# A two-block sequence model on one core: twelve column units of the second projection by Strassen's seven products, and a recurrence moved beside the row blocks

## The chip, the cores and the metric

The kernel runs on one core of a Trainium2 chip, as one launch. The metric is the device time of that launch in microseconds (us), lower is better. Engine names are those of the profile: PE is TensorE, with PEld for its weight loads, DVE is VectorE, ACT is ScalarE, POOL is GpSimd and SP is SyncE, which here only issues DMAs.

## What is computed

Two blocks run one after the other on 2048 tokens of width 1024, in float32. The first is a pooling mixer with a residual and two norms. The second, where the change lies, projects its normed and modulated input `h` to 4624 columns and feeds two mixers:

```python
proj = h @ w_in + b_in                       # (2048 x 1024) @ (1024 x 4624)
(na_q, na_k, na_v, na_z, ml_q, ml_k, ml_v, ml_o, ml_z,
 i_f, f_f, i_b, f_b) = split(proj)           # nine blocks of 512 columns and 16 gate columns
na_out = neighbourhood_attention(na_q, na_k, na_v, rpb) * silu(na_z)
mq, mk = silu(short_conv(ml_q, ml_k))        # five taps along the tokens
h_fwd = mlstm_chunkwise(mq, mk, ml_v, i_f, f_f)
h_bwd = flip(mlstm_chunkwise(flip(...)))
y = concat(na_out, norm((h_fwd + h_bwd) * sigmoid(ml_o)) * ml_norm_w * silu(ml_z)) @ w_out
```

`mlstm_chunkwise` carries a state from chunk to chunk: `C_new = decay * C + v_c^T k_c`. That is the recurrence of the title.

## The kernel before

There is no scheduler. Each engine has a program written out by hand, one Python method for each engine of each stage (`sp`, `act`, `dve`, `pool`, `pe`), and the engines meet by counting semaphores: `w.wait_ge(*self.full.ge(n + 1))` holds the engine that runs it, and all that stands behind it on that engine. An engine's instructions run in the order in which they are written.

**Products.** Every float32 operand is held as a high and a low part, and each product of 128 x 128 x 512 takes three matmuls (`mm3`, L143, matmuls L145 to L147): high by high, high by low, low by high.

**The second projection** (`Proj`, L1209). `self.work` is the list of its items, one PSUM bank each. The nine blocks go by names: nq, nk, nv, nz for the attention, mq, mk, mv, mo, mz for the other mixer. A block of 512 columns is four units of 128 columns. An item is either one unit by 512 tokens, or, for the row blocks mv, nv and mo, all four units by 128 tokens (16 items for a block). Both take 8 x 3 = 24 matmuls of 512 columns. The order is nq, nk, mv, mk, mq, the 16 gate columns, nv, nz, mz, mo. Items before `nv0` use eight PSUM banks in turn, later ones five; the other three belong to the recurrence. Units of weights sit in six slots in SBUF. `load` (L1371, on SP) brings a unit's raw weights into one of two buffers `iraw`, `split_high` (L1403, ACT) and `split_low` (L1440, DVE) make its two parts, and a unit's loads stand in `after[n]`, behind the item `n` that frees its slot.

**Reading out.** DVE adds the bias to a row item (L1653, `row_step`). For mq and mk ACT adds the bias and DVE runs the five taps (L1618). Items of nv are stored by SP itself: it waits for the item's `row_step` and then issues four DMAs into `VM`, or six into `VM` and `VE` at every second item (L1496, L1498). All other stores are POOL's.

**The recurrence** (`States`, L2249) has 31 steps, one after each item from `s0` on. In step s, SP loads a chunk of keys into the one buffer `skC` (L2312, once the last chunk was transposed) and of values into `sv` (L2322), and stores the state of step s - 2 (L2327). POOL weighs the values (L2378), PE multiplies (L2397) and, in the first 16 steps, transposes the keys (L2409), and DVE updates the state (L2358). Before it come the `Gates` steps (L2111), which begin at `g0`. PE's part after item n is, cut:

```python
s = n - self.s0 - 1                       # product of the step before
... w.wait_ge(*self.weighed.ge(i + 1)) ... matmuls L2397
s += 1                                    # transposes of this step
if 0 <= s < NT:
    w.wait_ge(*self.k_in.ge(s + 1))       # keys of step s = n - s0 have landed
    ... four transposes L2409
```

and SP's part after item n issues the load of step s = n - s0, behind whatever SP does for item n of the projection. In the kernel before, `g0 = nv0 + 3` and `s0 = nv0 + 21`: the 31 steps stand beside items 5 to 15 of nz, all of mz and the first items of mo.

The attention (`Attention`, L1770) starts inside the last item of mo with the work of its first two pairs (`first_pe`, `first_act`, `first_dve`, `first_pool`); its inputs are loaded beside mo (`early_sp`, L1864), and POOL prepares its masks there (`block`, L2010).

Of the kernel before, what the change touches and what calls it, by code (L numbers as in the profile page):

```python
# [10 lines left out]
P = 128  # L11
# [1193 lines left out]
BLOCKS = [("nq", 0), ("nk", 1), ("mv", 6), ("mk", 5), ("mq", 4), ("nv", 2), ("nz", 3), ("mz", 8), ("mo", 7)]  # L1205
# [3 lines left out]
class Proj:  # L1209


    NU = 6
# [3 lines left out]
    def __init__(self, k, banks, out, gw):  # L1216
        self.k, self.out, self.gw = k, out, gw
        NU = self.NU
# [9 lines left out]
        self.cu = [k.at(f"cu{i}", 168 + 2.03125 * i, [P, 4 + W + 2]) for i in range(2)]  # L1228
        self.ca = [k.at(f"ca{i}", 172.0625 + 2.03125 * i, [P, W + 2]) for i in range(2)]
        self.br, self.wgr = k.at("br", 178.125, [P, 2, W]), k.at("wgr", 182.125, [P, KT, 16])  # L1230

        self.wg = k.at("wg", 176.125, [P, KT, 48], F32R)
# [8 lines left out]
        self.conv_u, self.conv_out, self.row_step, self.sign = k.sem("conv_u"), k.sem("conv_out"), k.sem("row_step"), k.sem("sign")  # L1241
# [3 lines left out]
        self.cols = [b * W + j * P for _, b in BLOCKS for j in range(4)]  # L1245
        work = []
        for bi, (name, b) in enumerate(BLOCKS):
            u0 = 4 * bi
            if name == "nv":
                work += [("gates", 0, tb) for tb in range(TB)]  # L1250
            if name in ROW_BLOCKS:
                work += [(name, u0, m) for m in range(NT)]
            elif bi == 0:
                work += [(BLOCKS[u // 4][0], u, tb) for tb in range(TB) for u in range(NU)]
            else:
                units = range(u0 + 2, u0 + 4) if bi == 1 else range(u0, u0 + 4)
                work += [(name, u, tb) for u in units for tb in range(TB)]
        self.work = work

        jobs = [("h", 0, 0), ("h", 0, 1), ("h", 0, 2), ("h", 0, 3), ("w", 0), ("w", 1)]  # L1260
        self.early = {12: (0, 2), 13: (2, 4), 14: (4, 5), 15: (5, 6)}
        self.ahead, self.after, nu = {}, {}, NU
        for n, (name, u, tb) in enumerate(work):
            first = len(jobs)
            if n == 0:
                jobs += [("w", 2), ("w", 3)]
            elif n < 3:
                jobs.append(("w", n + 3))
            if 2 <= n < 6:
                jobs.append(("h", 1, n - 2))  # L1270
            if n == 3 * NU:
                jobs.append(("gates",))
            if NU <= n < 3 * NU and u < 4:
                jobs.append(("h", tb + 1, u))
            self.ahead[n] = (first, len(jobs))
            first = len(jobs)
            last_of_unit = name not in ROW_BLOCKS and name != "gates" and tb == 3
            last_of_rows = name in ROW_BLOCKS and tb == NT - 1
            more = u + 1 + NU if last_of_unit else u + 4 + NU if last_of_rows else 0
            while nu < min(more, 36):  # L1280
                jobs.append(("w", nu))
                nu += 1
# [5 lines left out]
        self.freed = {}  # L1288
        for n, (name, u, tb) in enumerate(work):
            if name == "gates":  # L1290
                continue
            for x in range(4 if name in ROW_BLOCKS else 1):
                self.freed[u + x] = n + 1


        self.stage, nst, self.convs = {}, 0, {}
        for n, (name, u, tb) in enumerate(work):
            if name in ("mq", "mk"):
                self.convs[n] = len(self.convs)
            else:  # L1300
                self.stage[n] = nst
                nst += 2 if name in ("nq", "nk") else 1
        self.users = {}
        for n, i in self.stage.items():
            self.users[i] = n
            if work[n][0] in ("nq", "nk"):
                self.users[i + 1] = n

        self.evac_at, self.row_at, self.sign_at, c = {}, {}, {}, 0
        for n, (name, u, tb) in enumerate(work):  # L1310
            c += {"nq": 4, "nk": 1, "nz": 1, "mz": 1, "gates": 1, "mo": 1}.get(name, 0)
# [152 lines left out]
    def sp(self, e, att, states):  # L1464
        k, io, out, work = self.k, self.k.io, self.out, self.work
        w = Waits(e)
        for n, (name, u, m) in enumerate(work):
# [31 lines left out]
            for x in range(*self.after[n]):  # L1499
                self.load(e, w, x)  # L1500
# [1611 lines left out]
```

## Time and profile before

| | |
|---|---|
| runs | 1884.83, 1886.8 and 1890.14 us, median 1886.8 |
| span of the profiled execution | 1883.3 us (the page gives no other time of it; the median of the runs is 3.5 us longer) |
| busy: PE, PEld, DVE, ACT, POOL | 99%, 82%, 52%, 33%, 29% of the span |
| granted PE clock | 0.999 of full speed over the span |
| first projection item to last | from 598 to 1442 us of the span |
| waits of PE for another engine | 12, the longest 1.8 us |

A busy share is the part of the span in which an engine had an instruction running. In a view of waits, "A <- B" says that engine A sat idle until B's instruction released it. In the chain of work each piece is what the next one waited for. A DMA's "to landing" is from its issue to its data being there.

### The profile page before, as it was taken

How to read it: one execution, taken by the hardware profiler on the slowest of the kernel's cores; microseconds unless marked ns; L12 is line 12 of the kernel's file. 1: busy time of each engine (PE TensorE's matmuls, PEld its weight loads, DVE VectorE, ACT ScalarE, POOL GpSimd, SP SyncE). 2: the span in 40 equal slices, each digit the busy share in tenths (PEclk: the TensorE clock that was granted, in tenths of full speed). 3: DMA queues.
4: the chain of work that ended last, by engine and by line, in shares of the span. 5: the costliest groups of instructions: out<-in, count | busy, mean ns of one | idle time of the engine just before them, and what ended most of it. 6: DMA issues, size and time to landing. Idle time of an engine off the chain costs nothing.

```text
span 1883.3 us, 26698 instructions
## 1 busy us (share of the span) xinstructions
PE 1865.6 (99%) x10035; PEld 1540.4 (82%) x10035; DVE 982.4 (52%) x2117; ACT 618.3 (33%) x1317; POOL 552.5 (29%) x925
## 2 busy tenths in 40 slices
PE   9999999999999999999999999999999999999998
PEld 8888878888888888888888787888887777788886
DVE  6556565775666433114777322223213777776665
ACT  7321111233444432101222202221114667655552
POOL 2112222233642222110110000222314777544442
PEclk9999999999999999999999999999999999999999
DMA  6223142366897745312221123665563776867663
GB/s 197 95 79 119 62 128 81 104 184 235 306 266 252 235 168 162 101 50 84 74 78 68 53 62 116 211 211 171 168 220 105 243 232 224 271 219 241 230 229 112
DMA packets 236365, 303.55 MB, mean 161 GB/s; under 512 B 41414, under 2 KB 161126, under 8 KB 236204
## 3 DMA queue, kind: packets, MB, share of 16 engines
q1 hardware_dynamic: 205724, 215.84, 37.4%
q0 software_dynamic: 23600, 77.61, 11.4%
q10 hardware_dynamic: 6912, 8.39, 1.2%
q8 instruction: 80, 1.31, 0.3%
q14 instruction: 49, 0.40, 0.1%
HBM read 194.71 MB, written 107.54 MB: 160 GB/s over the span
## 4 chain that ended last, share of the span: by engine, by line
PE 94%; DVE 2%; DMA 2%; issue 1%; ACT 1%; POOL 0%; SPq 0%; POOLq 0%; DVEq 0%; ACTq 0%
PE banks L145 25%; PE banks L147 25%; PE banks L146 25%; PE banks L2106 3%; PE banks L2069 3%; PE banks L2088 3%; PE banks L2704 2%; PE banks L2706 1%; PE banks L2397 1%; DMA iraw<-in_w_in 1%; PE banks L2089 1%; PE banks L2674 1%; PE banks L234 1%; PE banks L1109 1%; PE banks L1741 0%
## 5 line engine op out<-in xcount | busy, mean ns | idle before, releaser
L145 PE MATMUL banks<-hT,wu 128*128 128x512 f32 (+1 forms) x528 | 204.6, 387 | 1.1 <-DVE wu L512 0.6
L147 PE MATMUL banks<-hT,wu 128*128 128x512 f32 (+1 forms) x528 | 202.3, 383 | 0.0
L146 PE MATMUL banks<-hT,wu 128*128 128x512 f32 (+1 forms) x528 | 202.2, 383 | 0.0
L145 PE MATMUL banks<-iT,wub 128*128 128x512 f32 x384 | 151.2, 394 | 0.0
L145 PE MATMUL banks<-iT,wua 128*128 128x512 f32 x384 | 150.8, 393 | 0.0
L145 PE MATMUL banks<-wub,iT 128*128 128x512 f32 x384 | 150.6, 392 | 0.0
L147 PE MATMUL banks<-iT,wub 128*128 128x512 f32 x384 | 149.7, 390 | 0.0
L147 PE MATMUL banks<-iT,wua 128*128 128x512 f32 x384 | 149.5, 389 | 0.0
L146 PE MATMUL banks<-wub,iT 128*128 128x512 f32 x384 | 149.5, 389 | 0.0
L147 PE MATMUL banks<-wub,iT 128*128 128x512 f32 x384 | 149.5, 389 | 0.0
L146 PE MATMUL banks<-iT,wua 128*128 128x512 f32 x384 | 149.5, 389 | 0.0
L146 PE MATMUL banks<-iT,wub 128*128 128x512 f32 x384 | 149.4, 389 | 0.0
L1653 DVE TENSOR_TENSOR st<-banks,br 128x512 f32<-128x512 f32 x48 | 33.1, 692 | 201.0 <-PE banks L147 193.5
L145 PEld LDWEIGHTS banks<-hT,wu 128*128 128x128 f32 x528 | 99.3, 188 | 25.3 <-ACT ub L470 4.3
L147 PEld LDWEIGHTS banks<-hT,wu 128*128 128x128 f32 x528 | 99.2, 188 | 19.6
L146 PEld LDWEIGHTS banks<-hT,wu 128*128 128x128 f32 x528 | 99.3, 188 | 18.5
L1932 ACT ACTIVATE p<-s,ast 128x480 f32<-128x480 f32 (+1 forms) x128 | 83.7, 655 | 53.0 <-DVE ast L1970 53.0
L145 PE MATMUL banks<-ws,ys 128*128 128x512 f32 x256 | 100.5, 393 | 0.0
L147 PE MATMUL banks<-ws,ys 128*128 128x512 f32 x256 | 99.8, 390 | 0.0
L146 PE MATMUL banks<-ws,ys 128*128 128x512 f32 x256 | 99.7, 389 | 0.0
L1618 DVE SCALAR_TENSOR_TENSOR ca<-cu,cw,ca 128x512 f32<-128x512 f32 (+2 forms) x128 | 96.3, 752 | 4.5
L2039 POOL TENSOR_SCALAR p<-p,ast 128x384 f32<-128x384 f32 (+1 forms) x128 | 71.9, 562 | 46.2 <-DVE ast L1976 44.8
(293 smaller groups left out, 4116.3 us busy)
## 6 DMA issues: line engine op xcount, KB each, us to landing
iraw<-in_w_in SPq DMA_DIRECT2D x36, 512.0 KB, 4.4
wa<-in_w_ada SPq DMA_DIRECT2D x48, 256.0 KB
yT<-sg POOLq DMA_DIRECT2D x32, 256.0 KB, 3.1
oraw<-yT SPq DMA_DIRECT2D x32, 256.0 KB, 4.8
xr<-in_x SPq DMA_DIRECT2D x16, 512.0 KB, 4.4
h<-h POOLq DMA_DIRECT2D x16, 512.0 KB, 4.3
hT<-tr POOLq DMA_DIRECT2D x16, 512.0 KB, 5.1
tws<-wg SPq DMA_DIRECT2D x16, 512.0 KB, 5.1
```

What stands on the lines that cost most here:

```text
L145: e.matmul(ps, lh, rh, start=first, stop=False)
L146: e.matmul(ps, lh, rl, start=False, stop=False)
L147: return e.matmul(ps, ll, rh, start=False, stop=last)
L234: t = e.transpose(self.tp[m][g][:, j * P:(j + 1) * P], self.x[m][:, (4 * g + j) * P:(4 * g + j + 1) * P], self.ident[:])
L1618: e.scalar_tensor_tensor(out=a[:, left:right], in0=cur[:, left + x:right + x], scalar=cw[:, x, ch:ch + 1], in1=a[:, left:right], op0=ALU.m ...
L1653: e.tensor_tensor(self.st[i % 2][:], pb, self.br[:, x % 2, :], ALU.add).then_inc(*self.row_step.inc())
L1932: e.activation(self.pr[n % 8][:, 0:N], self.sr[n % 4][:, 0:N], ACT.Exp, bias=self.st[:, n, 0:1], scale=-1.0, accum_out=self.st[:, n, 1:2]) ...
L2039: e.tensor_scalar(rows[:, :, 0:P], rows[:, :, 0:P], self.st[:, n, 2:3], 1.0, ALU.mult, ALU.mult).then_inc(*self.scaled.inc())
L2069: t = e.matmul(self.pS[(2 * p + hh) % 4][:, 0:N], b[r, q, (2 * i + a) * P:(2 * i + a + 1) * P], keys, start=x == 0, stop=x == 2)
L2088: e.transpose(self.pT[x][:, j * P:(j + 1) * P], probs[:, 160 * j:160 * j + P], self.ident[:])
L2106: t = e.matmul(self.pO[d, 0:P], v, self.ptr[(2 * q + hh) % 4][r, j * P:(j + 1) * P], start=(j == 0), stop=(j == nb))
L2704: t = e.matmul(o, self.eb[c % 2][d][:, h, :], self.v1[c % 2][:, h, :], start=True, stop=not self.inter(c, d))
```

## The change

It does three things.

1. **Order of the projection.** A table `PLAN` gives the units' order: nz first (with the gate columns after each group of four items), then mk, mq, mv, mq, nv, mq, mo. nq, nk and mz, twelve units together, leave the list, which is now 100 items long. The weight slots follow a table `SLOT`.
2. **The recurrence** begins one item after mv begins (`g0`), its steps 18 items later (`s0`): item 63 and on, so beside the last item of mq2 (items 60 to 63), nv (64 to 79), mq3 (80 to 83) and mo (84 to 99, up to item 93).
3. **Fast**, a new class. nq, nk and mz are taken as 2 x 2 blocks (two halves of the inner dimension, two units, two token blocks of 512) and multiplied by Strassen's seven products, each 12 matmuls of 512 columns; there are 84 products in 6 rounds of 14. Three of the sums of weights and three of the sums of tokens are made in DRAM: SP copies one operand to `wsum` or `hsum`, and POOL issues a DMA that adds the other (15 of each). The other sums, and the high and low parts, are made on DVE and ACT. Attention's early work moves to the last products.

```diff
+PLAN = [("nz", 0), ("nz", 1), ("nz", 2), ("nz", 3), ("mk", 0), ("mk", 1), ("mk", 2), ("mq", 0), ("mq", 1), ("mk", 3),
...
+        work = [x for tb in range(TB) for x in [(PLAN[u][0], u, tb) for u in range(4)] + [("gates", 0, tb)]]
+        for u in range(4, len(PLAN)):
+            name, j = PLAN[u]
             if name in ROW_BLOCKS:
+                work += [(name, u, m) for m in range(NT) if j == 0]
             else:
+                work += [(name, u, tb) for tb in range(TB)]
...
-        self.nv0 = nv0 = next(n for n, x in enumerate(work) if x[0] == "nv")
-        self.place = [n % 8 if n < nv0 else (nv0 + (n - nv0) % 5) % 8 for n in range(len(work))]
+        self.g0 = g0 = next(n for n, x in enumerate(work) if x[0] == "mv")
+        self.place = [n % 8 if n < g0 else (g0 + (n - g0) % 5) % 8 for n in range(len(work))]
...
     def sp(self, e, fast, states):
...
             if name == "nv":
                 i = self.stage[n]
...
                 w.wait_ge(*self.row_step.ge(self.row_at[n]))
                 for y in range(2):
...
                         e.dma_start(k.VM[:, 40 * r4:40 * r4 + nc, m // 2, a, :].rearrange("hp c d -> c hp d"), src).then_inc(*self.v_st[i % 2].inc())
...
             for x in range(*self.after[n]):
                 self.load(e, w, x)
+            fast.copy(e, w, n - 22)
             states.sp(e, w, n)
             if name == "mo":
-                att.early_sp(e, w, m)
+                fast.early_sp(e, w, m)
...
             out.tail_pool(e, w, n)
+            fast.add(e, w, n - 36)
             states.pool(e, w, n)
...
+class Fast:
+    N, ND, OUTS, SLOTS = 84, 6, 48, 10
+    SEQ = [(i, q) for i, q in ((5, 0), (5, 1), (2, 0), (2, 1), (1, 0), (3, 0), (1, 1), (3, 1), (4, 0), (4, 1), (6, 0), (6, 1), (7, 0), (7, 1))]
+    DOUBLES = [(("nq", 0), ("nk", 0)), (("nq", 2), ("nk", 2)), (("mz", 0), ("mz", 2))]
+    ORDER = [(0, 0), (0, 1), (0, 2), (1, 2), (1, 0), (1, 1)]
...
+    def copy(self, e, w, n):
+        if 0 <= n < 9:
+            b, x = divmod(n, 3)
+            e.dma_start(self.ws[b, x], self.columns(b, (0, 0, 1)[x], 0)).then_inc(*self.copy_in.inc())
+        elif 9 <= n < 15:
+            half, x = divmod(n - 9, 3)
+            e.dma_start(self.hs[half, x], self.tokens(half, self.LEFT[self.LONG[x]][0])).then_inc(*self.copy_in.inc())
+
+    def add(self, e, w, n):
+        if 0 <= n < 9:
+            b, x = divmod(n, 3)
+            w.wait_ge(*self.copy_in.ge(15))
+            e.dma_start(self.ws[b, x], self.columns(b, (1, 0, 1)[x], 1), accum_op=ALU.add).then_inc(*self.added.inc())
...
+    def early_act(self, e, w, m):
+        if m in self.early_x:
+            self.tokens_high(e, w, *self.early_x[m])
+        if m == NT - 1:
+            for j in range(4):
+                self.weights_high(e, w, j)
...
+    def act(self, e, att):
+        for j in range(self.N):
...
+            elif j in self.at:
+                self.high(e, w, self.at[j])
+            if j + 4 < self.N:
+                self.weights_high(e, w, j + 4)
...
+    def pe(self, e, att):
+        for j in range(self.N):
...
+            for c in range(KT // 2):
+                e.matmul(ps, t[:, 0, c], x[:, 0, c], start=new and c == 0, stop=False, skip_group_check=not new)
+                e.matmul(ps, t[:, 0, c], x[:, 1, c], start=False, stop=False, skip_group_check=not new)
+                m = e.matmul(ps, t[:, 1, c], x[:, 0, c], start=False, stop=c == KT // 2 - 1, skip_group_check=not new)
+            m.then_inc(*self.full.inc())
...
     def early_sp(self, e, w, m):
-        if m == 11:
-            w.wait_ge(*full)
+        if m == 80:
+            w.wait_ge(*fast.full.ge(m))
             for j in self.jobs:
                 if j[0] == "t":
                     self.load(e, w, 0, j)
...
-        self.g0 = proj.nv0 + 3
-        self.s0 = proj.nv0 + 21
+        self.g0 = proj.g0 + 1
+        self.s0 = self.g0 + 18
```

How the order of instructions moves shows at three places. First, the program of SP beside the recurrence. `skC` and `sv` are its loads of keys and values, `CD` the store of the state. Before, with nz and mz as the items:

```order
L2312 DMA skC_158<-mk 128x4x128 [waits s_turned_236]
L2322 DMA sv_160<-mv 128x4x128 [waits s_weighed_238]
L2327 DMA CD<-state_162 128x516 [waits updated_240]
L1389 DMA iraw_178_134<-in_w_in 128x8x128 [waits i_lo_208]
L2312 DMA skC_158<-mk 128x4x128 [waits s_turned_236]
```

and now, beside two items of nv (L1490 and L1492 are the stores that were L1496 and L1498, L2742, L2752 and L2757 the recurrence):

```order
L1490 DMA VM<-st_189_145 40x4x128 [waits row_step_217]
L1490 DMA VM<-st_189_145 40x4x128
L1490 DMA VM<-st_189_145 8x4x128
L1492 DMA VE<-st_189_145 32x512
L1490 DMA VM<-st_189_145 8x4x128
L1492 DMA VE<-st_189_145 32x512
L2742 DMA skC_158<-mk 128x4x128 [waits s_turned_235]
L2752 DMA sv_160<-mv 128x4x128 [waits s_weighed_237]
L2757 DMA CD<-state_162 128x516 [waits updated_239]
L1490 DMA VM<-st_188_144 40x4x128 [waits row_step_217]
L1490 DMA VM<-st_188_144 40x4x128 x3
L2742 DMA skC_158<-mk 128x4x128 [waits s_turned_235]
```

The load of keys stood behind waits of the recurrence and of weight buffers; it now stands behind the wait for the current item's row add and that item's stores. Second, PE at the end of an item of nv in the change:

```order
L147 MATMUL banks<-wub_133,iT_172_128 128x512
L2825 MATMUL banks<-swv_161,skT_159 128x129 [waits updated_239,kt_out_236,s_weighed_237]
L2825 MATMUL banks<-swv_161,skT_159 128x129
L2825 MATMUL banks<-swv_161,skT_159 128x129 [waits updated_239]
L2825 MATMUL banks<-swv_161,skT_159 128x129
L2837 MATMUL banks<-ident_58,skC_158 128x128 [waits sk_in_229]
L2837 MATMUL banks<-ident_58,skC_158 128x128 x3
L145 MATMUL banks<-wub_133,iT_172_128 128x512 [waits biased_212]
```

The order on PE is that of before, with a row item in the place of a column item: the product of one step, then the transposes of the next, then the next item. Third, SP behind the last item of nv in the change (L1382 loads a unit of weights; before, four such loads stood there too, and no `sv` behind them):

```order
L1492 DMA VE<-st_189_145 32x512
L1382 DMA iraw_178_134<-in_w_in 128x8x128 [waits i_lo_208]
L1382 DMA iraw_179_135<-in_w_in 128x8x128 [waits i_lo_208]
L1382 DMA iraw_178_134<-in_w_in 128x8x128 [waits i_lo_208]
L1382 DMA iraw_179_135<-in_w_in 128x8x128 [waits i_lo_208]
L2752 DMA sv_160<-mv 128x4x128 [waits s_weighed_237]
```

The values for the recurrence's next product are loaded behind four loads of weights, two of which wait for buffers.

## Rows read from the trace of the kernel before

**Rows 1.** The page's head, the busy line of PE and the granted clock
```profile
span 1883.3 us, 26698 instructions
PE 1865.6 (99%) x10035; PEld 1540.4 (82%) x10035; DVE 982.4 (52%) x2117; ACT 618.3 (33%) x1317; POOL 552.5 (29%) x925
PEclk9999999999999999999999999999999999999999
```

**Rows 2.** Windows: PE, PEld, DVE, ACT, POOL busy, clock, DMA share, GB/s
```profile
600.00:615.00 15.00, 13.98 (x70) 11.50 (x69) 10.26 (x13) 8.65 (x16) 2.74 (x5) 1.00 1.06 353
900.00:1000.00 100.00, 100.00 (x443) 82.81 (x442) 72.34 (x123) 26.77 (x42) 10.50 (x19) 1.00 0.21 72
1140.00:1165.00 25.00, 23.24 (x104) 18.93 (x103) 6.48 (x9) 7.48 (x8) 1.33 (x3) 1.00 0.50 141
```

**Rows 3.** Timeline of DVE in nv: start, duration, and idle before with its releaser
```profile
1064.36 0.69 DVE L1653 TENSOR_TENSOR st<-banks,br 128x512 f32<-128x512 f32 x1 [4.75 <-PE banks L147]
1069.79 0.69 DVE L1653 TENSOR_TENSOR st<-banks,br 128x512 f32<-128x512 f32 x1 [4.75 <-PE banks L147]
```

**Rows 4.** Chain of work, window 1140 to 1170: start, duration, piece
```profile
1142.22 0.25 PE banks L147
1142.49 0.70 DVE st L1653
1143.21 0.27 SPq L1496
...
1145.06 0.32 SPq L1498
1145.42 0.42 SPq L1389
1145.88 5.25 DMA iraw<-in_w_in
1151.16 1.07 ACT wub L1438
1152.26 1.24 DVE wub L1443
1153.51 4.35 DMA iraw<-in_w_in
1157.88 1.07 ACT wub L1438
1158.98 1.23 DVE wub L1443
```

**Rows 5.** Timeline of SP in nv, an item with four DMAs
```profile
1070.51 1.54 SPq L1496 DMA_DIRECT2D VM<-st  x4
1072.21 1.15 SPq L2134 DMA_DIRECT2D I<-gt  x2
```

**Rows 6.** Line L2312, the load of keys: issue in ns min/median/max, and to landing
```profile
L2312 SPq DMA_DIRECT2D skC<-mk x16: 359/360/372, 1169.8 to 1273.6; - x16
...
DMA to landing us min/median/max: 2.5/3.2/3.8
```

**Rows 7.** Chain of work, whole span: two products of the recurrence
```profile
1183.70 0.89 PE banks L2397 x8
1190.52 0.89 PE banks L2397 x8
```

**Rows 8.** Timeline of POOL: a wait for values, and their weighing
```profile
1199.74 1.05 POOL L2378 TENSOR_TENSOR swv<-sv,wT 128x516 f32<-128x516 f32 x1 [0.79 <-DMA sv<-mv]
```

**Rows 9.** Line L2322, the load of values: issue in ns, and to landing
```profile
L2322 SPq DMA_DIRECT2D sv<-mv x30: 529/530/1432, 1170.2 to 1370.9; - x30
...
DMA to landing us min/median/max: 3.0/3.4/4.8
```

**Rows 10.** PE's waits, 1100 to 1180, and the page's group of conv taps
```profile
PE banks L2240 <- DVE dg L2213: 1.8, 1, 1.8
...
L1618 DVE SCALAR_TENSOR_TENSOR ca<-cu,cw,ca 128x512 f32<-128x512 f32 (+2 forms) x128 | 96.3, 752 | 4.5
```

**Rows 11.** DMA issues: count, KB each, median us to landing
```profile
rpbp<-in_rpb POOLq DMA_DIRECT2D x1, 465.0 KB, 4.5
...
mv<-st POOLq DMA_DIRECT2D x16, 256.0 KB, 2.3
```

**Rows 12.** Timelines of ACT, POOL, SP and PE where the attention takes over
```profile
1436.27 0.63 ACT L1578 ACTIVATE st<-st 128x512 f32<-128x512 f32 x1 [4.81 <-DVE st L1653]
1436.91 1.28 ACT L1932 ACT_TABLE_LOAD   x1
...
1437.73 1.92 POOL L2017 COPY mid<-tab 128x960 f32<-128x960 f32 x2
1439.71 3.12 POOL L2024 MEMSET mid<- 32x640 f32 x7
...
1419.21 4.47 SPq L1852 DMA_DIRECT2D tab<-Z  x8
...
1443.05 1.59 PE L2069 MATMUL banks<-hd 64*128 64x480 f32 x12 [0.78 <-DVE st L1653]
```

More of the change, by code:

```diff
@@ L1287, in __init__ @@
         self.rawn = {n: i for i, n in enumerate(n for n, j in enumerate(jobs) if j[0] != "gates" and n not in self.passing)}
[L1288 to L1296, printed above, removed]
+        self.stage, self.convs = {}, {}
         for n, (name, u, tb) in enumerate(work):
@@ L1300, in __init__ @@
             else:
[L1301 to L1309, printed above, removed]
+                self.stage[n] = len(self.stage)
+        self.users = {i: n for n, i in self.stage.items()}
+        self.evac_at, self.row_at, c = {}, {}, 0
         for n, (name, u, tb) in enumerate(work):
-            c += {"nq": 4, "nk": 1, "nz": 1, "mz": 1, "gates": 1, "mo": 1}.get(name, 0)
+            c += name in ("nz", "gates", "mo")
             self.evac_at[n] = c
@@ L1429, in split_high @@
             u = j[1]
-            if u >= self.NU:
-                w.wait_ge(*self.full.ge(self.freed[u - self.NU]))
+            if self.prior[u] is not None:
+                w.wait_ge(*self.full.ge(self.freed[self.prior[u]]))
             elif u >= 2:
@@ L1472, in sp @@
                     self.pass_load(e, w, 1, x)
-            if n == 5:
+                w.wait_ge(*out.modulated.ge(NT))
+                e.dma_start(self.wgr[:], self.win[:, :, 36 * P:36 * P + 16]).then_inc(*self.wg_in.inc())
+            if n == 4:
                 for x in range(4):
@@ L1542, in act @@
                 else:
-                    w.wait_ge(*out.modulated.ge(NT))
+                    w.wait_ge(*self.full.ge(self.freed[1]))
                 e.activation(cu[:, 4:4 + W], pb, ACT.Identity, bias=bc[:, bcol:bcol + 1]).then_inc(*self.biased.inc())
@@ L1891, in sp @@
         proj, states = self.proj, self.states
-        w.wait_ge(*proj.full.ge(len(proj.work)))
+        w.wait_ge(*self.fast.full.ge(self.fast.N))
         for i in range(2):
             w.wait_ge(*proj.ca_st[i].ge(16))
-        for name in ("mv", "mz", "mo"):
+        for name in ("mv", "mo"):
             proj.stored_all(w, name)
-        w.wait_ge(*proj.row_step.ge(48))
+        self.fast.stored(w, self.fast.OUTS)
+        self.fast.read(w)
         states.stored_all(w)
@@ L2295, in sp @@
         if n == self.g0 - 1:
-            for i in range(2):
-                w.wait_ge(*proj.ca_st[i].ge(16))
             proj.stored_all(w, "gates")
@@ L2362, in pool @@
         if n == self.g0 - 1:
-            for i in range(2):
-                w.wait_ge(*self.proj.ca_st[i].ge(16))
             self.g.consts(e, w)
@@ L2383, in pe @@
             for b in self.proj.reserved:
-                self.proj.read_out(w, max(x for x in range(self.proj.nv0) if self.proj.place[x] == b))
+                self.proj.read_out(w, max(x for x in range(self.proj.g0) if self.proj.place[x] == b))
         self.g.pe(e, w, n - self.g0)
@@ L2995, in whole @@
         mixer = Mixer(k, hT, banks, norm)
+        over = [x for x in k.used[first:] if x not in (mixer.full, mixer.y_step)]
         out = FirstOut(k, banks, mixer, ident, mhalf)
         gw = GatedWeights(k, out)
-        ended = k.used[first:]
+        ended = [x for x in k.used[first:] if x not in over]
         proj = Proj(k, banks, out, gw)
         states = States(k, proj, ident)
-        att = Attention(k, proj, states, ident)
         with k.nc.Block() as block:
```

602 lines of the change are left out of this document (472 added, 130 removed).

## The prediction

> **What bounds the kernel now.** The page's first lines come first: PE is busy for 1865.6 of 1883.3 us and its clock is full in every slice, while the next engine, DVE, reaches 52% [rows 1]. So time goes only where PE does less, or where it is made to wait. The windows say where it waits in the projection: never in the conv items, where DVE is busy for 72 of 100 us; 1.0 us at the start and 1.8 us behind nv [rows 2]. The reader is to see that PE is the whole bound and that any wait of PE adds its full length. Next comes PE's pace: the row adds of two successive items of nv start 5.43 us apart [rows 3], 24 matmuls, so 0.226 us a matmul.
>
> The last view decides this case. The chain of work behind the last item of nv runs: last matmul ends (1142.47), DVE adds the bias, SP issues six stores, and only then the next load, at 1145.42 [rows 4]. SP's program is in order: what stands behind a row item's stores starts 2.95 us after the item's last matmul. Today nothing that PE needs soon stands there for nv.
>
> **The change part by part.** Twelve units took 12 x 4 x 24 = 1152 matmuls, the 84 products take 1008; all have 512 columns. 144 fewer at 0.226 us: **-32.6 us**. The rest of PE's work is the same and in another order.
>
> *Keys beside nv.* PE, after item n, multiplies the last step's product and then transposes keys that SP loads in its part for the same item n. Beside nz and mz, SP had no wait for item n and the load came an item early. Beside nv it stands behind the wait for item n's row add and behind its stores. From the last matmul's end: 0.02 and 0.70 for the row add, 0.02 to SP, together 0.74 [rows 4]; then six DMAs in 2.21 us (1143.21 to 1145.42), or four in 1.54 [rows 5] and a gap of 0.05; the keys' own issue 0.36 and 3.2 to land [rows 6]. That is 5.9 us for items with four stores and 6.5 with six. PE has the product to do meanwhile, 0.89 us [rows 7]. It then stands still for 5.0 or 5.6 us. Keys are transposed in steps 0 to 15, after items 63 to 78; item 63 is not a row item, so 15 items of nv pay: 8 x 5.0 + 7 x 5.6 = **+79.2 us**. With the landing's extremes, 2.5 and 3.8 [rows 6], this is 69 to 88. No other wait of the recurrence hides or doubles it: the state's store goes out 1 us after the keys and DVE has the longer item to update in. Behind SP's wait also stand the values; they are needed an item later and are covered.
>
> The page "DMA: Bandwidth & Descriptors" of the Trainium skill (Anatomy of one DMA) fits 2.0 us + bytes / 436e3 to DMAs that GpSimd issues; for 256 KB that would be 2.6 us, not the 3.2 of the row, and by an estimate from that page the sum would be 9 us lower. The keys are issued by SP, beside other traffic, and the row is this very load, so the sum goes by the row.
>
> *Values behind nv.* After nv's last item SP also issues four weight loads; the fourth starts 11.04 us after the last matmul (1153.51), since it waits for a buffer [rows 4]. The values of the next product stand behind it in SP's program: issue 0.53, landing 3.0 to 4.8, where I take 4.8 because two loads of 512 KB are in flight [rows 9], weighing 1.05 [rows 8]. They are ready at 11.04 + 0.05 + 0.53 + 4.8 + 1.05 = 17.5; PE has finished item 80 at 5.4. **+12.0 us** (10 to 13). ACT and DVE are held by the same four units, and the conv item behind them ends at about 22, just before PE asks for the next update.
>
> *Gates.* Their last product now follows the second conv item behind mv. DVE, which must first read out the product before, has four units to split (two need a fresh load of 4.35 to 5.25 us, then 1.07 and 1.24 [rows 4]), to about 11.5, and a conv of five taps of 0.75 [rows 10], to 15.6; PE is there at 10.9. 4.7 in the place of today's 1.8 at this spot: **+2.9** (0 to 5).
>
> *Start of Fast.* The first weights are split behind the last item's row add and sigmoid: 0.70 + 0.63 + about 0.63 + 0.70 [rows 4, 12]: **+2.7**.
>
> *Handover.* The last output takes add, high, low, two issues and a landing of 2.3 [rows 11], about 5.5 us after the last product, and the first copies of the attention wait for it. The tables are asked for only three products before the last (4.47 of issues, then masks of 1.92 + 3.12 on POOL [rows 12]), which ends about when the last product does. Bounds 0 and 8; I take **+4**, since the store alone is 3 us later than the 0.78 that PE waits today [rows 12].
>
> *First gate columns.* They now follow the fourth item, 25 us in, and their weights wait for the last modulated tile: 0 to 4, **+2**.
>
> *Inside Fast.* A product lasts 12 x 0.226 = 2.7 us. DVE has about 0.7 a product for weights and as much for an output; where the token halves change, seven low parts and two sums of 2048 columns come in, 2.5 us each at twice the 1.24 of 1024 [rows 4]: some 37 us of DVE in 13 products of 35. Four products of lead cover it nearly: 0 to 10, **+3**.
>
> *DRAM sums.* 15 copies on SP and 15 adds on POOL in a stretch with 0.21 of the DMA engines in use [rows 2]; first used 37 items later. 0, as long as POOL's queue keeps up (a rival).
>
> Sum: -32.6 + 79.2 + 12.0 + 2.9 + 2.7 + 4 + 2 + 3 = +73. The profiled span of 1883.3 becomes 1956.5, the median of 1886.8 (3.5 above it) **1960**. That is slower, because some twenty waits outweigh a saving of 1.7%.
>
> **Rivals.**
> *The adds clog POOL's queue.* No row shows an accumulating DMA. The nearest, a DRAM to DRAM copy of 465 KB, lands in 4.5 us [rows 11]. If an add holds the queue for 4.5 (512 KB) and 9 us (1 MB), the backlog over one item's 5.4 us each is 6 x 3.6 = 22 us, which two staging buffers and five banks (some 23 us) absorb. If it holds it twice as long, 9 x 3.6 + 6 x 12.6 = 108, and 85 reach PE during mv: 1960 + 85 = 2045. For it: an add reads two operands. Against it: the 4.5 has a landing in it, not only transfer. The page "Collectives: The Full Stack" of the Trainium skill (Part 3) says that a reduce reads two sources and runs at half the rate of a copy; by that rule this is the case that comes. 10%.
> *Fast starves.* An output's staging buffer is free again after some 7.5 to 12 us, three buffers allow 8.1. With token parts in between it may be 4 us late per three outputs, 7 or so per round beyond PE's lead: 6 x 7 = 40, 2000 us. 8%.
> *A smaller wait.* Half the price beside nv, from a load that lands sooner or stores that issue faster: 1920. 5%.
> *Faster.* If SP were not held by the row, as with a count one item lower in its wait, keys and values would be there in time and both big terms fall: 1886.8 - 32.6 + 14.6 = 1869. It decides at 18 us in both terms together, about 0.4 us an item. Against it stands the order of SP's program, where each load of keys follows a wait for the current row add. 4%.
> That the change does not do what it says is out: the order shows the 144 matmuls gone.
>
> **How the numbers follow.** The forecast has 73%, its own range 1935 to 1990 (low and high ends of the terms). Adding the starving case and the upper edge gives 1930 to 2010; the clog, the faster case and most of the smaller wait are left out, some 18%. A measurement can tell about 0.3% from no change: faster 4%, same 2%, slower 94%.
>
> **What the profile after would show.** Right: PE idle some 5 us before each of 15 groups of transposes (L2837) in nv, put down to the load of keys; a single wait of about 12 us before the product after item 80; PE busy about 1833 us; Fast near 228 us. Wrong: no wait at L2837, or idle time on PE in mv with POOL's stores landing late, or gaps inside Fast.

## The result, and the profile after

The changed kernel takes 2045.0 us (median of 4 runs, 2043.1 to 2051.4), before 1885.9 in the same comparison: a ratio of 1.085, with a 95% interval of 1.083 to 1.087. It is slower, as forecast, but by 159 us where 73 were forecast, and outside the range. The profiled execution took 2043.1 with a span of 2041.3, so the difference to explain is one of spans: 2041.3 - 1883.3 = 158.0 us. Some runs of the experiments below fell into a slower state of the chip (one of four of joined_tables with 2065 us, two of four of states_first with 2091 and 4773 us, and with them the profiles of these two) and are left out of every time given.

The head of the page of the changed kernel, against [rows 1]:

```profile
span 2041.3 us, 26803 instructions
...
PE 1887.9 (92%) x9891; PEld 1548.2 (76%) x9891; DVE 1092.0 (53%) x2231; ACT 689.0 (34%) x1390; POOL 571.9 (28%) x940
...
PE   9999999999998999999666679999799799999998
...
PEclk9999999999999999999877889999899799999999
```

Three things are to be seen. PE runs 144 instructions fewer (9891 for 10035), as the change says. It stands idle for 2041.3 - 1887.9 = 153.4 us, where it was 17.7. And it is *busy* for 22.3 us longer with less work: the clock row is no longer full. So 158.0 is 135.7 of new idle time and 22.3 of busy time, where the prediction had -32.6.

PE's waits in the whole run (engine, line and its releaser: us in total, times, longest):

```profile
PE banks L2837 <- DMA skC<-mk: 69.9, 15, 5.2
PE banks L2825 <- POOL swv L2806: 16.6, 4, 12.8
PE banks L1109 <- ACT tr L957: 8.5, 2, 7.8
PE banks L2501 <- DVE fso L2069: 8.1, 1, 8.1
PE banks L2187 <- DVE fpart L2112: 6.8, 1, 6.8
PE banks L2187 <- issue: 6.5, 2, 3.7
PE banks L2656 <- DVE L L2612: 4.7, 1, 4.7
PE banks L2520 <- DVE pt L2424: 4.1, 1, 4.1
PE banks L2672 <- DVE mpB L2650: 3.9, 1, 3.9
PE banks L2501 <- DMA hd<-nkl: 3.3, 1, 3.3
```

The first two are the prediction's two large terms, at their place: the 15 waits for keys, and the 12.8 for values. Of the others, the 3.9 is the prediction's wait of the gates and one of the two of "issue" its start of Fast (2.7); the rest it had smaller or not at all.

Windows of PE alone (length, busy, matmuls, granted clock, DMA share, GB/s): two stretches beside nv, the one behind nv, Fast, and the handover.

```profile
978.00:1080.00 102.00, 65.76 (x270) 0.80 0.35 106
1080.00:1180.00 100.00, 66.35 (x275) 0.81 0.31 94
1180.00:1210.00 30.00, 17.25 (x74) 0.77 0.55 160
1322.00:1582.00 260.00, 241.98 (x1024) 0.95 0.68 208
1582.00:1600.00 18.00, 6.17 (x26) 0.59 0.34 110
```

What the clock means is told by single rows: the end of one item of nv, the wait, and the next item's first matmuls (start, length, what it is, idle time before it):

```profile
1165.46 0.39 PE L147 MATMUL banks<-wub,iT 128*128 128x512 f32 x1
1165.68 1.05 PE L2825 MATMUL banks<-swv,skT 128*128 128x129 f32 x8
1171.65 0.76 PE L2837 MATMUL banks<-ident,skC 128*128 128x128 f32 x4 [4.91 <-DMA skC<-mk]
...
1173.06 0.63 PE L147 MATMUL banks<-wub,iT 128*128 128x512 f32 x1
1173.49 0.63 PE L145 MATMUL banks<-wub,iT 128*128 128x512 f32 x1
```

Behind the wait the matmuls start 0.427 us apart, where they start 0.227 apart elsewhere, the spacing of 512 columns at 1.2 and at 2.4 GHz. Spacings of 0.40 to 0.45 us between matmuls of 512 columns occur 148 times from 600 us on and cost 148 x 0.2 = 30 us; 86 of them stand behind the 15 waits for keys, 3 to 8 behind each. The page "TensorE: Matmul & The Clock Gate" of the Trainium skill (Part 1) describes this: a PE that has stood idle is passed half of its clock's pulses until it has been busy for a while. The rows agree in both levels. The item's period is 13.6 us beside the 6.8 of before: 4.7 of wait and some 2.1 more, of which the slow spacings counted above make 1.1; the rest lies at the stop's two ends and was not split further.

SP's own rows in the same item (its queue: start, time to issue, transfer):

```profile
1166.60 1.54 SPq L1490 DMA_DIRECT2D VM<-st  x4
1168.19 0.38 SPq L2742 DMA_DIRECT2D skC<-mk  x1
1168.61 0.50 SPq L2757 DMA_DIRECT2D CD<-state  x1
```

Four stores, then the keys at 1168.19, and PE's transposes 3.46 us later: the chain is the one that was worked out. The load itself lands after 2.9 us (median; 2.7 to 3.4), a little sooner than the 3.2 of [rows 6], so it is not the load that got slower.

### The profile page after: what moved, and what is told of

It is laid out like the page before. It is cut to its first block, busy times and chain, and to the rows that moved or that the text cites. A ratio compares the mean times of both kernels' runs of the same rounds, so it can differ in the third digit from the quotient of the medians.

```text
span 2041.3 us, 26803 instructions
## 1 busy us (share of the span) xinstructions
PE 1887.9 (92%) x9891; PEld 1548.2 (76%) x9891; DVE 1092.0 (53%) x2231; ACT 689.0 (34%) x1390; POOL 571.9 (28%) x940
## 4 chain that ended last, share of the span: by engine, by line
PE 35%; DMA 6%; issue 3%; SPq 3%; DVE 3%; ACT 2%; POOL 1%; POOLq 0%; DVEq 0%
PE banks L145 5%; PE banks L146 5%; PE banks L147 5%; PE banks L2538 3%; PE banks L2187 2%; PE banks L2188 2%; PE banks L2189 2%; PE banks L2501 2%; PE banks L2520 2%; DMA skC<-mk 2%; PE banks L3132 1%; DMA sv<-mv 1%; PE banks L3134 1%; SPq L1490 1%; DMA tab<-Z 1%
## 5 line engine op out<-in xcount | busy, mean ns | idle before, releaser
L145 PE MATMUL banks<-wub,iT 128*128 128x512 f32 x384 | 163.3, 425 | 0.0
L146 PE MATMUL banks<-wub,iT 128*128 128x512 f32 x384 | 158.7, 413 | 0.0
L147 PE MATMUL banks<-wub,iT 128*128 128x512 f32 x384 | 157.6, 410 | 0.0
L2187 PE MATMUL banks<-fx,ft 128*128 128x512 f32 x336 | 135.2, 402 | 14.7 <-DVE fpart L2112 6.8
L2188 PE MATMUL banks<-fx,ft 128*128 128x512 f32 x336 | 134.2, 399 | 0.0
L2189 PE MATMUL banks<-fx,ft 128*128 128x512 f32 x336 | 134.0, 399 | 0.0
L2788 DVE SCALAR_TENSOR_TENSOR state<-state,dcB,banks 128x129 f32<-128x129 f32 x112 | 31.5, 345 | 128.4 <-DMA CD<-state 128.4
L2806 POOL TENSOR_TENSOR swv<-sv,wT 128x516 f32<-128x516 f32 x30 | 32.6, 1088 | 217.8 <-DMA sv<-mv 217.5
L145 PEld LDWEIGHTS banks<-wub,iT 128*128 128x128 f32 x384 | 78.7, 205 | 16.7 <-issue 0.4
L147 PEld LDWEIGHTS banks<-wub,iT 128*128 128x128 f32 x384 | 77.8, 203 | 17.7
```

Source lines behind the costliest of these rows:

```text
L145: e.matmul(ps, lh, rh, start=first, stop=False)
L146: e.matmul(ps, lh, rl, start=False, stop=False)
L147: return e.matmul(ps, ll, rh, start=False, stop=last)
L2187: e.matmul(ps, t[:, 0, c], x[:, 0, c], start=new and c == 0, stop=False, skip_group_check=not new)
L2188: e.matmul(ps, t[:, 0, c], x[:, 1, c], start=False, stop=False, skip_group_check=not new)
L2189: m = e.matmul(ps, t[:, 1, c], x[:, 0, c], start=False, stop=c == KT // 2 - 1, skip_group_check=not new)
```

## The experiments

Each was timed side by side with the kernel before, whose median was 1884.5 to 1886.4 us in these comparisons. The edits are to the changed kernel. The times were taken in four comparisons on different chips, apart from the one that gave 2045.0. The 95% interval of each ratio is about 0.17% or 3 us to either side, so a difference of 5 or 6 us from the changed kernel is hardly clear of noise, and one of 9 us is.

**1. The keys ahead of the row's wait.**

```
             if name == "nv":
                 i = self.stage[n]
+                if m == 0:
+                    states.sp(e, w, n)
+                if m < 15:
+                    states.sp(e, w, n + 1)
...
-            states.sp(e, w, n)
+            if not (64 <= n <= 79):
+                states.sp(e, w, n)
```

> SP issues the recurrence's part of item n+1 ahead of its wait for item n's row add, in nv's items; everything else stays. If the wait comes from SP's order (my theory), the 15 waits of PE for the load of keys (69.9 us in the profile of the changed kernel) go, and with them the stretches at the half clock behind each (row matmuls 0.427 us apart for about 10 of 24, some 2 us an item, 30 us): 2045 - 70 - 30 = 1945 us, granted clock 1.0 in nv. If SP's order is right but the clock is low for another reason than the waits, only 70 go: 1975, and the clock in nv stays at 0.8. If the load is late by traffic or by its own length, the waits stay: 2030 to 2045.

Measured: 1947.5 us, ratio to before 1.032 (1.030 to 1.034), so 97.5 less than the changed kernel. In the list of PE's waits the line for the keys is gone; the largest is now the other one:

```profile
PE banks L2830 <- POOL swv L2811: 16.9, 3, 13.7
PE banks L2506 <- DVE fso L2074: 12.7, 1, 12.7
```

SP's rows show the new order, with the next item's keys ahead of a row's stores, and PE's transposes without a wait:

```profile
1045.17 0.39 SPq L2747 DMA_DIRECT2D skC<-mk  x1
...
1047.87 1.43 SPq L1494 DMA_DIRECT2D VM<-st  x3
...
1051.35 0.60 PE L2842 MATMUL banks<-ident,skC 128*128 128x128 f32 x4
```

The window from 978 to 1080 us has a clock of 0.98 and PE busy for 99.62 of 102. So SP's order was the cause of 69.9 us of waiting, and 97.5 - 69.9 = 27.6 us more had been paid beside it. The two profiles agree: PE's busy time falls by 26.8 us (1887.9 to 1861.1) for the same matmuls. (Its idle time falls by 65.9 and not 69.9, mainly because the wait at the handover is 12.7 here for 8.1.) The rival of late traffic falls, since the DMA engines are now busier there (0.65 of them for 0.35) and the waits are gone.

**2. The waits stay, but PE works in them.**

```
             if s >= 1:
                 w.wait_ge(*self.kt_out.ge(s))
+                for x in range(19):
+                    e.matmul(self.pT, self.proj.wb[:, 0, 0, x % KT, :], self.proj.hT[0][:, 0, x % KT], start=True, stop=True)
             w.wait_ge(*self.k_in.ge(s + 1))
```

> The waits stay, but PE fills each of the 15 with 19 matmuls of 512 columns into the bank that the transposes overwrite (4.3 us of the 4.7 at full clock; extra work, nothing reads it). If the half clock is caused by PE standing still, the clock is 1.0 in nv, the item's period falls from 13.6 us to about 11.6, and the time by 25 to 32 us to about 2017, though 285 matmuls were added. If the clock was low for another reason, the fillers run at 0.427 us too, each item gets 3 to 4 us longer and the time is 2090 to 2105.

Measured: 2023.1 us (1.073, 1.071 to 1.075), 21.9 *less* with 285 matmuls more. One item:

```profile
1038.37 4.57 PE L2834 MATMUL banks<-iT,wub 128*128 128x512 f32 x19
...
1043.64 0.66 PE L2841 MATMUL banks<-ident,skC 128*128 128x128 f32 x4 [0.71 <-DMA skC<-mk]
1044.37 0.39 PE L146 MATMUL banks<-wub,iT 128*128 128x512 f32 x1
1044.60 0.40 PE L147 MATMUL banks<-wub,iT 128*128 128x512 f32 x1
```

Its remaining waits for the keys:

```profile
PE banks L2841 <- DMA skC<-mk: 7.9, 12, 0.9
```

The fillers and the row's matmuls behind the wait run at full speed, and the clock of the window is 0.99. This separates the two costs that experiment 1 removed together: standing still is what lowers the clock. The fillers last 14 x 4.57 + 5.39 = 69.3 us (the first group is slower, behind a stop of 2.4 us), and with the waits 69.3 + 7.9 = 77.2 us where the waits alone were 69.9. So 7.3 of the gain were used up, and 21.9 + 7.3 = 29.2 came back, close to the 27.6 of experiment 1. PE's busy time without the fillers, 1930.4 - 69.3 = 1861.1 us, is that of experiment 1.

**3. Single causes of the other waits.** Four edits, each alone.

*Values.* The four weight loads behind nv's last item go one to an item:

```
-            while nu < len(PLAN) and self.freed[self.prior[nu]] <= n + 1:
+            while nu < len(PLAN) and self.freed[self.prior[nu]] <= n + 1 and (n < 79 or len(jobs) == first):
```

> The four weight loads behind nv's last item are issued one an item (79 to 82) instead of all at 79. If the values of the next product wait behind them in SP's program, the wait of 12.8 us before the product after item 80 falls to about 1 to 3, with the slow matmuls behind it (0.77 of the clock in that stretch, 2 us): 2045 - 12 = 2033. If POOL or the load itself is late, the wait stays and the time is 2045. A loss is possible if mo then waits for its weights: up to 2055.

Measured: 2039.9 us (1.082, 1.081 to 1.084), only 5 less, which is not clear of noise; the waits have to tell. This one falls from 12.8 to 4.0, but DVE, which now has a split in each conv item, updates the state late: PE's waits on the state, 2.8 us in the changed kernel, become

```profile
PE banks L2825 <- DVE state L2788: 7.5, 4, 3.1
```

SP's order was the cause of most of the 12.8, and behind it stood the next wait.

*The first gate columns.*

```
-                w.wait_ge(*out.modulated.ge(NT))
-                e.dma_start(self.wgr[:], ...)
+            if n == 1:
+                w.wait_ge(*out.modulated.ge(NT))
+                e.dma_start(self.wgr[:], ...)
```

> SP's wait for the last modulated tile and the load of the gate columns move from item 0 to item 1, behind the load of the fifth unit. If that wait held the unit's load back, and ACT behind it, which PE's transposes wait for, the 7.8 us of PE at 617.85 go: 2045 - 8 = 2037. If ACT is late for its own work, or PE then waits for the gate columns instead, nothing: 2042 to 2046.

Measured: 2033.9 us (1.079, 1.077 to 1.080), 11.1 less. In the changed kernel ACT stands for 9.8 us on weights whose load SP issued only behind this wait (ACT's waits from 598 to 640 us, of the changed kernel):

```profile
ACT wub L1431 <- DMA iraw<-in_w_in: 13.9, 3, 9.8
```

and PE's last transposes need ACT. With the edit PE is busy for 22.00 of the 22 us from 598 to 620 (19.14 before the edit), and for all of the 95 behind them (89.34). So the wait is gone; a part of the 11.1 may be chance, since the wait before the gates' fourth step, which this edit does not touch, is 2.2 here and 2.5 to 4.8 in the other runs that keep the adds beside mv.

*The adds.* They are left out, and their readers wait for the copies (this kernel computes something else and serves only to be timed):

```
-            fast.add(e, w, n - 36)
-            w.wait_ge(*self.added.ge(15))
+            w.wait_ge(*self.copy_in.ge(15))
```

> The 15 accumulating DMAs are left out (the DRAM sums hold only their first terms, so three of the seven products are made from other numbers); their readers wait for the copies instead. If the adds clog POOL's queue (my rival, 2045), mv's row adds no longer wait for late stores (39.4 us of DVE in the changed kernel's profile), and what of it reaches PE goes: the 4.7 us before the gates' fourth step at L2656 and its slow matmuls, 2045 - 6 = 2039, at most 2030. If the adds are free as forecast: 2045, and the 4.7 stays.

Measured: 2039.2 us (1.081, 1.079 to 1.083), 5.8 less, at the edge of noise. DVE's waits for mv's staging buffers between 700 and 980 us, first in the changed kernel, then without the adds:

```profile
DVE st L1608 <- DMA mv<-st: 39.4, 8, 8.9
```

```profile
DVE st L1608 <- DMA mv<-st: 5.0, 1, 5.0
```

The adds do clog the path of mv's stores, but 39.4 us of DVE became one wait of PE, the 4.7 before the gates' fourth step, which is gone here (and also in best_joined below, where the 1 MB adds stand elsewhere). From 819 to 866 us, beside nine adds of 512 KB, PE was busy for 47.00 of 47 us in the changed kernel: DVE's waits did not reach it. So the rival's mechanism exists, at about a fifteenth of its price (5.8 of 85).

*Inside Fast.*

```
-        self.late_x = {..., 34: (1, 5), 36: (1, 2), 37: (1, 3), 39: (1, 1), 41: (1, 4), 44: (1, 6), 46: (1, 7)}
+        self.late_x = {..., 34: (1, 5), 36: (1, 2), 38: (1, 1), 40: (1, 3), 43: (1, 4), 46: (1, 6), 49: (1, 7)}
...
-        if m == NT - 1:
+        if m == 12:
             for j in range(4):
                 self.weights_high(e, w, j)
```

> Inside Fast alone: the first four weights are split after mo's item 12 rather than behind its last row, and the token parts of the second half are spread (products 34, 36, 38, 40, 43, 46, 49 instead of 34 to 46). If DVE's queue causes the gaps, the 2.7 us at Fast's start, the 3.7 at 1449.9 and the 6.8 at 1467.2 go with their slow matmuls: 2045 - 13 - 4 = 2028. If only the start goes: 2041. If the late parts of the last two become the wait: 2045 or up to 2050.

Measured: 2035.7 us (1.079, 1.078 to 1.081), 9.3 less, about half of what was expected. The start's wait goes and the 6.8 becomes 2.9, but 3.8 us stay on a low part of weights (L1911). DVE is not full there: from 1410 to 1480 us it was busy for 46.9 of 70 us in the changed kernel and for 46.3 with the edit. It stands waiting for ACT's high parts, first in the changed kernel (1400 to 1480 us):

```profile
DVE ft L1911 <- ACT ft L1906: 20.2, 13, 2.8
```

and for 19.3 us with the edit, while ACT waits in turn for DVE's sums and outputs. Which of these steps sets the remaining 3.8 was not tested.

*The handover.* The queries' loads start at product 72, the bias tables go ahead of nz and the values:

```
-        if m == 74:
+        if m in (72, 74):
...
-                if j[0] == "q":
+                if j[0] == "q" and j[1] // 2 == (m - 72) // 2:
...
-        if m == 78:
...
         if m == 80:
...
                 if j[0] == "t":
                     self.load(e, w, 0, j)
+            for j in self.jobs:
+                if j[0] in ("z", "v"):
+                    self.load(e, w, 0, j)
```

> The loads of the handover alone (queries from product 72, tables ahead of nz and the values at product 80), on the changed kernel. If the tables wait for the transfers queued before them, the 8.1 us wait of PE for the attention's first pairs falls to about 2 to 4 and the half clock behind it shortens: 2045 - 7 = 2038. If the tables' own transfers are the cause: 2044.

Measured: 2034.2 us (1.079, 1.077 to 1.081), 10.8 less. The waits of the handover fall from 17.5 to 8.2 us. In the changed kernel the tables land after 8.3 us (median), at most 16.8; with the edit after 4.2, at most 7.0; before, after 2.8, at most 5.0. DVE's row tells that the 8.1 us, which the list puts down to DVE, end with a table: DVE stands until the table is there and then works off four tiles and the output for which PE waits.

```profile
1587.74 0.49 DVE L2400 CUSTOM_DVE_ANT_0 s<-banks,tab 128x320 f32<-128x320 f32 x1 [5.24 <-DMA tab<-Z]
```

So the tables were late because of what was queued before them.

**4. Can the waits be taken away together?** Experiments 1 and 3 without the last, and then with it:

> keys_ahead, values_spread, gate_columns_later and fast_spread together. If their gains are of separate waits they add up: 2045 - 97 - 11 - 15 (the values' wait of 13.7 and its clock) - 16 = 1906, granted clock 0.99 or more in every stage. If the waits are one chain, with the next one showing up behind each that goes, 1920 to 1930. Before is 1884.5, and it stays faster unless all of it and more comes back.

> joined, and three loads moved: the values of step 17 also ahead of nv's last row; the first head's queries start two products before its keys (at product 72, not 74); the bias tables go ahead of nz and the values of the neighbourhood attention at product 80. If the 12.7 us of PE at the handover come from the tables queued behind 6 MB of other loads, they fall to about 5: 1906 - 8 - 3 = 1895. If the tables are late by their own eight transfers, 1903; if the attention then waits for its values, 1906 to 1910.

Measured: joined 1919.4 us (1.018, 1.016 to 1.019), joined_tables 1907.4 (1.012, 1.010 to 1.014), 12.0 less where 11 were expected of the three moved loads. The four edits of joined save 97.5 + 5.1 + 11.1 + 9.3 = 123.0 one by one and 125.6 together, so within the noise the savings add up. It is 13 us short of the expectation because two edits give less than was set for them, here as alone: values 5.1 for 15, Fast 9.3 for 16. For the values the reason is seen again: behind nv the wait on POOL's values has fallen to 2.4 us and this has come for it:

```profile
PE banks L2832 <- DVE state L2795: 7.1, 3, 2.9
PE banks L2832 <- DVE state L2792: 6.3, 1, 6.3
```

DVE's rows in the stretch say why (start, length, what, idle before): a conv, a split, and only then the state.

```profile
1081.00 3.10 DVE L1601 SCALAR_TENSOR_TENSOR ca<-cu,cw,ca 128x510 f32<-128x510 f32 x4
1085.74 2.07 DVE L1436 TENSOR_TENSOR wub<-iraw,wub 128x1024 fp32r<-128x1024 f32 x1 [1.64 <-ACT wub L1431]
1087.73 0.88 DVE L2792 COPY state<-banks 128x129 f32<-128x129 f32 x4
```

**5. The state first on DVE: a miss.** On joined_tables, from item 59 on:

```
+            if n >= 59:
+                states.dve(e, w, n)
             if name in ("mq", "mk"):
```

> joined_tables, and from item 59 on DVE updates the recurrence's state ahead of the item's own conv or row add and its weight splits. If the 13.4 us of PE on the state (6.3 at item 80, then 2 to 3 each) come from the split that stands before the update in DVE's program, they go with 2 us of clock: 1910 - 15 = 1895. If DVE is simply full in these items (conv 3.7, split 2.1, state 1.1, bias copies, of 5.4 us an item), PE waits elsewhere, for a bank or for mo's weights: 1903 to 1910.

> states_first, and: the four weight loads behind mv one an item as well; the six 1 MB adds moved from mv to nv, where POOL stores nothing; the token parts of Fast's second half one or two products later. If these waits (4.8 before the gates' fourth step, 3.8 before the sixteenth, 3.8 and 2.0 in Fast) are each of the cause named, 1895 - 12 = 1883, which is before's time; a saving of 32.6 us is then nearly used up by handover, Fast and slower clock. If they return elsewhere: 1890 to 1895.

Measured: states_first 1937 and 1941 us (ratio 1.029, 1.027 to 1.031), best_joined 1956.1 (1.037, 1.035 to 1.039). Both are slower than joined_tables, by 32 and 49 us. In best_joined PE waits in other places:

```profile
PE banks L2833 <- POOL swv L2814: 31.4, 13, 5.8
```

and DVE, from 950 to 1230 us, stands on the store of the state, with the item's conv or row add now queued behind it:

```profile
DVE state L2796 <- DMA CD<-state: 160.4, 25, 13.3
```

The state's update waits until SP has stored the last one. Behind the conv, in joined, DVE stood on that store for 31.3 us in the same window. Ahead of the conv, the wait closes a ring. POOL weighs values from 1104.65 to 1105.72 us; SP, which waited for it, loads the next values at 1105.75 and only then stores the state; and then:

```profile
1106.32 0.62 SPq L2765 DMA_DIRECT2D CD<-state  x1
...
1109.95 1.13 DVE L2796 SCALAR_TENSOR_TENSOR state<-state,dcB,banks 128x129 f32<-128x129 f32 x4 [3.13 <-DMA CD<-state]
...
1115.90 0.58 POOL L1638 DMA_DIRECT2D mq<-ca  x1 [10.18 <-ACT ca L1545]
...
1116.50 1.06 POOL L2814 TENSOR_TENSOR swv<-sv,wT 128x516 f32<-128x516 f32 x1
```

The state waits for the store, the conv for the state, POOL's store of the conv for the conv, and the next weighing for POOL's store: 11.85 us from one weighing to the next. These rows are of best_joined. That states_first is slow for the same reason is inferred, since no profile of it can be used; and how much of best_joined's further 17 us comes from the adds beside nv was not separated.

**6. The state between the two.** The state goes behind the conv and ahead of the splits; mv's weights one to an item; Fast's parts of best_joined; adds as in the changed kernel. All of it is on joined_tables.

```
             out.tail_dve(e, w, n)
+            if n >= 59:
+                states.dve(e, w, n)
             for x in range(*self.after[n]):
                 self.split_low(e, w, x)
-            states.dve(e, w, n)
+            if n < 59:
+                states.dve(e, w, n)
```

> joined_tables, and from item 59 on DVE updates the state after the item's conv or row add but ahead of the weight splits (states_first had it ahead of both and took 1937 to 1941); the four weight loads behind mv one an item; the token parts of Fast a product or two later; the adds stay where they are. If the state's wait of 6.3 and 7.1 us comes from the splits alone, it goes, and so does the 3.8 before the gates' sixteenth step: 1910 - 13 - 4 - 2 = 1891. If the order on DVE is a chain with the store of the state, as states_first suggests, 1905 to 1915. Before's 1885.7 is out of reach of this step unless Fast's own gaps go too.

Measured: 1898.7 us beside 1885.2 for before (1.007, 1.006 to 1.009), between the two forecasts (1891, and 1905 to 1915). It is 8.7 less than joined_tables, and the shares of the three edits in this were not separated. Its page begins:

```profile
span 1893.1 us, 26803 instructions
...
PE 1848.5 (98%) x9891; PEld 1520.8 (80%) x9891; DVE 1091.4 (58%) x2231; ACT 687.8 (36%) x1390; POOL 573.5 (30%) x940
```

146 of the 159 us are gone, with every product of the change in place, and it is still 0.7% slower than before. Its idle time is 44.6 us (17.7 before), its busy time only 17.1 less than before's, 15.5 short of the 32.6. About 6 us of these go to some 30 slow spacings behind the waits that are left; the rest was not measured apart. The largest waits left are 5.7 at the handover, 4.3 behind nv and 3.7 in Fast. No version that beats before was found.

## Why the prediction was right and wrong

**The fewer matmuls, -32.6: right in number, wrong as a sum.** The 144 are gone and the pace at full clock is still 0.227. The step that failed is the one that priced everything after it: "24 matmuls, so 0.226 us a matmul", held for the whole run, and "any wait of PE adds its full length", and no more. The page of before showed a full clock in every slice, but also an engine that never stopped for long. What the runs show instead: a wait of some 5 us adds its length and a stretch at half the clock behind it. PE's busy time came out at 1887.9 where 1833 was forecast: 55 of the 85 us that were missed, and without them the time would have been 1990, inside the range. Experiments 1 and 2 show 27 of the 55 for the 15 waits beside nv (PE's busy time for the same matmuls falls by 26.8 in both); the remaining 28 were not measured apart. With the clock in it, each wait beside nv would have cost 4.7 + 1.8 (27.6 / 15) instead of 5.3.

**Keys, +79.2: the wait right, its price not.** 15 waits, 69.9 us, the longest 5.2; the bounds were 69 to 88. It lies at their low end since the load landed after 2.9 us for 3.2, and the first of the 15 was only 2.0, behind a wait of 2.4 for the first values. The mechanism was shown by taking it away.

**Values, +12.0: right.** 12.8, with 3.8 more in three other waits for values that were not forecast. That the conv item would end "just before PE asks for the next update" was too close: with the wait removed, the state on DVE stood right behind it.

**Gates, +2.9: right at its place, another missed.** 3.9 against the forecast 4.7; but the adds brought 4.7 at an earlier step (2.2 to 4.8 from run to run).

**DRAM adds, 0: wrong, small.** 5.8 by experiment. The time of 2045 is that of the clog rival to the microsecond, which is chance: the mechanism gave 5.8 of its 85 us. The 1 MB adds land after 15.0 us and the 512 KB ones after 9.3 (median), so the rival had their length about right (twice 9 and twice 4.5). What failed in it is that an add holds the queue for that long: the 1 MB adds were issued 4 to 9 us apart and each landed some 15 us after its issue, so two or three were on their way at once. mv's stores, queued among them, landed after 7.2 us for the 2.3 of [rows 11], and hardly any of that reached PE.

Whether the rule of the page "Collectives: The Full Stack" (Part 3) of the Trainium skill, half the rate for a reduce, holds for these adds is left open. The medians look alike, 14.7 for SP's plain copies of 1 MB and 15.0 for the adds:

```profile
L1849 SPq DMA_DIRECT2D hsum<-hT x6: 590/1197/6618, 744.7 to 758.3; - x6
...
DMA to landing us min/median/max: 7.9/14.7/18.9
...
L1860 POOL DMA_DIRECT2D hsum<-hT x6: 1043/1092/2235, 863.3 to 894.2; - x6
...
DMA to landing us min/median/max: 14.1/15.0/17.0
```

But six copies were issued within 14 us and queued behind one another, and the adds were spread over 31 us. The first copy, with none before it, landed after 7.9 us, about half of the quickest add (14.1); at 512 KB the quickest copy took 5.1 and the quickest add 7.2 (medians 7.3 and 9.3). No run issued both in the same way beside the same traffic.

**First gate columns, +2: undersized.** 7.8 of wait, 11.1 by experiment. The step looked at who reads the gate columns, and not at what stands behind their wait in SP's program: the fifth unit's weights, for which ACT, and so PE's transposes, waited. It is the very reading that found the keys, not made a second time.

**Start of Fast, +2.7: right**, 2.7. **Inside Fast, +3: undersized.** 3.7 and 6.8 of wait; "Four products of lead cover it nearly" took DVE's sum of work and not its order, with ACT and DVE waiting for each other in turn. The stage lasted 260 us where "near 228" was named, 242 of them busy. The rival of a starving Fast (40 us) did not come.

**Handover, +4: undersized.** 3.3 + 8.1 + 2.0 + 4.1 = 17.5 us. The step counted the issue of the tables and left out what was in flight before them, 4 MB of queries and keys and 2 MB of nz and values. Moving loads made the kernel 10.8 us faster.

In idle time, 105.8 us were forecast to be added (the sum of the terms without the matmuls) and 135.7 came; the 30 us are the gate columns, Fast, the handover, the gates' earlier step, the other waits for values and the state, less the 9 by which the keys came out below their term. With the 55 of the clock and of the stops, that is the 85.

## What to carry to other kernels

An engine's program here is a queue: a wait put into it holds everything behind it, so for each wait that a change adds, list what is issued after it until the next stage, and who needs each of these. Price a wait of PE at its length plus what the slow clock takes afterwards; here 4.7 us cost 6.5, and filling the wait with useless matmuls made the kernel faster. The saving in matmuls, 1.7%, was worth less than some twenty gaps of this kind, and moving the instruction that is waited for to the front closed a ring elsewhere (experiment 5).

## What the runs showed of the hardware

In the changed kernel a stop of PE of 4.3 to 5.2 us beside nv was followed by 512-column matmuls 0.427 us apart, 4 to 8 such spacings each time, and a stop of at most 0.9 us (fill_waits) by none. Between these the rows are mixed: 2.7 us at the start of Fast were followed by 7 slow spacings, 2.5 us before a product beside mo by none. Nineteen matmuls that nothing reads, put into each of 15 such stops, brought the clock from 0.80 to 0.99 and the time down by 22 us.

Accumulating DMAs of 1 MB from DRAM to DRAM, issued 4 to 9 us apart, landed after 14.1 to 17.0 us; plain copies of that size landed after 7.9 us (the first of six) to 18.9 us (queued behind others).
